# Two MoE routers: each tile of rows gets its own place on the way out, rows are turned first, the modulation's work comes behind, expert slots are shifted by three

## The chip, the cores and the metric

The kernel runs on one core of one Trainium2 chip, in one launch. The metric is device time in microseconds of the whole program. TensorE (PE), VectorE (DVE), ScalarE (ACT), GpSimd (POOL) and SyncE (SP) run programs of their own and meet at semaphores.

## The reference, cut to what matters

Two blocks in sequence. The first has two layers, each a mixer (Fourier and convolution; then attention) and a mixture of experts behind it; the second is one layer with two dense feed-forwards and a mixer between them. The change lies in the mixtures of experts:

```python
def hier_moe(h, grp_w, grp_b, exp_w, exp_b, w_gate, w_up, w_down):
    g_logit = (h @ grp_w) + grp_b                       # 4 groups
    g_idx = argmax(g_logit);  g_prob = softmax(g_logit)[g_idx]
    e_logit = ((h @ exp_w) + exp_b).reshape(n, 4, 8)[g_idx]
    top_v, top_i = lax.top_k(e_logit, 2)
    w = g_prob * softmax(top_v);  e_idx = g_idx * 8 + top_i
    return routed_experts(h, e_idx, w, w_gate, w_up, w_down)

# routed_experts: rows sorted by expert into blocks; per block
#   y = (silu(x @ w_gate[e]) * (x @ w_up[e])) @ w_down[e]
# and out[token] += weight * y
```

There are 768 rows (512 of x, 256 of ctx) in layer 0 and 512 in layer 1, each of 1024 float32; 32 experts, with gate, up and down weights of 1024 x 512 (2 MB each). Layer 1's modulation (scale, shift and gate vectors from `c`, twelve products with units of `mod_w[1]`) is needed only after layer 0, and its units 0 to 3 are computed inside layer 0's router.

## The kernel before, in words

**Layout.** The activations `hT` lie transposed: 8 tiles of 128 features by 768 (or 512) rows. Weights live in `ring`, six slots of 4096 columns (2 MB each); most of the rest is cut from `scr`. There are eight PSUM banks, taken in turn by `ps.take`: an instruction that fills a bank first waits (`ps.ready`) until what its last user left there was taken out.

**The router's job.** After the norm, `pe_router` multiplies `hT` by the router weights and turns the logits, and VectorE (`dve_router`) picks groups and experts, step by step on small tiles. It needs TensorE four more times: counts of rows per expert (`r_n`) and running counts (`r_k`) once the one-hot sum `aa` is there, a broadcast of the experts' places (`r_p`) once `by_expert` is there, and `r_r`, which turns one-hot tiles `oa` and `ob` into the list of rows of each block. From `r_r` VectorE makes `rt`, the row numbers by which POOL gathers.

**Rows on their way out.** Blocks read their rows from HBM, so each tile of 128 rows of `hT` (6 tiles in layer 0, 4 in layer 1) is transposed by TensorE into two banks (`rows(i)`, tag `r_h`), copied by ScalarE into one of two places in `M.hst` and sent by POOL to `hrows` in HBM (`pool_router`, 0.5 MB each). ScalarE copies tile i only when tile i - 2 has landed. When all tiles have landed and `rt` is there, POOL gathers the rows of blocks 0, 1 and 2 (`pool_rows`); TensorE's first transpose of a gathered tile (`x_tr(0)` in `pe_blocks`) begins the expert stage.

**Modulation in layer 0's router.** `mod_load(u)` brings two pieces of 1 MB (half a unit each) into two places of `scr`, each free when TensorE has used what was in it; `pe_mod_pieces` multiplies; ScalarE's `mod_row` copies the result, `pe_mod_turn` turns it in a bank of its own, ScalarE's `mod_columns` copies that. The third x place of the blocks lies over a piece's place, so POOL's gather for block 2 waits until unit 3 is done.

**Orders.** Each engine's program is an order written out by hand. In layer 0 TensorE does: pieces 0, logits, pieces 1, tiles 0 and 1, `r_n` and `r_k`, turn 0, pieces 2, `r_p`, tile 2, turn 1, tile 3, pieces 3, `r_r`, tiles 4 and 5, turns 2 and 3. Layer 1 is the same without the modulation. SP (`sp_moe`, one queue in order) waits for the end of the stage before, then loads router weights and, between the pieces, the fixed weights of expert blocks 0 and 1. Block b's gate, up and down go to slots (3b + kind) mod 6: block 0 has 0, 1, 2, block 1 has 3, 4, 5. From block 2 on POOL fetches weights by an indirect DMA, into slots that TensorE has freed. Ten blocks are wide (128 rows), among them 0, 1 and 3; the other 22 are narrow (64 rows).

**Slots in the stages before.** The Fourier mixer loads raw weights into slots 3, 4 and 5 (its last three jobs into 4, 5 and 3), and 0 to 2 hold tables and split activations to its end. Attention has scratch in slots 0 to 2, output weights in 3 and 4, and the modulation's units 4 to 11 in 5.

**Lines of the profile.** Operations go through small helpers, so the profile's lines are those of helpers: L92 matmul, L95 transpose, L98 and L102 activation and copy on ScalarE, L106 to L120 VectorE's forms, L132 a plain DMA, L135 a gather.

Of the kernel before, what the change touches and what calls it, by code (L numbers as in the profile page):

```python
# [272 lines left out]
def build(nc, I, out, upto=99):  # L273
# [21 lines left out]
    NSLOT, SLOT = 6, 4096  # L295
# [11 lines left out]
    hrows = nc.dram_tensor("hrows", (768, 1024), F32, kind="Internal").ap()  # L307
# [30 lines left out]
    def slot(s, a=0, n=SLOT):  # L338
        return ring[:, s * SLOT + a:s * SLOT + a + n]
# [199 lines left out]
    def pe_mod_turn(e, M, u):  # L539
        l = M.l  # L540
        o = ps.take("mod_t", l, u)
        e.wait_ge(*ps.ready("mod_t", l, u))
        e.wait_ge(*ps.emptied("mod", l, u))
        for j in range(4):
            m = e.matmul(o[:, 2 * j:2 * j + 2], M.row[M.units.index(u) % 2][:, 128 * j:128 * j + 128], group_sum, True, True)
        m.then_inc(*ps.fill("mod_t", l, u))
# [430 lines left out]
    router_in = signal("router_in")  # L977
# [60 lines left out]
                         M.T, None))  # L1038

    def expert_slot(kind, b):  # L1040
        return (3 * b + kind) % NSLOT

    def mod_piece(u, half):
        return lambda kt: moes[0].half[half][:, 512 * (kt % 4):512 * (kt % 4) + 512]

    def sp_moe(e, l):
        M = moes[l]
        e.wait_ge(*act_stage.of(("f", "at")[l]))
        e.wait_ge(*dve_stage.of(("f", "at")[l]))
        e.wait_ge(*ps.filled((st_f, st_at)[l].name, "sum"))  # L1050
        e.dma(M.wr.rearrange("p (k n) -> p k n", k=8), I["router_w"][l]).then_inc(*router_in.up(l, "w", by=16))
        e.dma(M.rb, I["router_b"][l]).then_inc(*router_in.up(l, "b", by=16))

        def fixed(b, *kinds):
            for kind in kinds:
                weights_load(e, expert_slot(kind, b), ("e", l, kind, b),
                             I[f"exp_{('gate', 'up', 'down')[kind]}{l}"].rearrange("(e p) n -> e p n", p=128)[b], 1, 4096)

        def mod_load(u):
            for half in range(2) if l == 0 else ():  # L1060
                wr.take(8 + half, "mod_piece", u, half)
                e.wait_ge(*wr.open("mod_piece", u, half))
                e.dma(M.half[half].rearrange("p (k n) -> p k n", k=4), I["mod_w"][1, u][:, 4 * half:4 * half + 4, :]
                      ).then_inc(*wr.load("mod_piece", u, half))
        mod_load(0)
        fixed(0, 0)
        mod_load(1)
        fixed(0, 1)
        mod_load(2)
        fixed(0, 2)  # L1070
        mod_load(3)
        fixed(1, 0, 1, 2)

        for b in range(FIXED, M.NB):
            for kind in range(3):
                wr.take(expert_slot(kind, b), "e", l, kind, b)
        e.wait_ge(*y_out[0].of(l, 30))
        e.wait_ge(*y_out[1].of(l, 31))
        e.wait_ge(*pool_step.of("further", l))
        for a, n in chunks(M.T):  # L1080
            for i in tiles_of(a, n):
                for q in range(2):
                    r = 768 * q + 128 * i
                    e.dma(moe_y(l, i, q), yrows[r:r + 128, :]).then_inc(*y_in[a].up(l, i, q, by=16))
# [8 lines left out]
    def pe_router(e, l):  # L1093
        M = moes[l]
        NT, T = M.NT, M.T
        if l == 0:
            pe_mod_pieces(e, 0)
        e.wait_ge(*router_in.of(l, "b"))

        for a, n in chunks(T):  # L1100
            o = ps.take("r_l", l, a)
            e.wait_ge(*ps.ready("r_l", l, a))
            for kt in range(8):
                e.wait_ge(*h_ready.of(("hm", l), kt))
                h = 64 * (kt % 2)
                m = e.matmul(o[h:h + 64, 0:n], M.wr[:, 64 * kt:64 * kt + 64], H(kt, a, n), kt < 2, kt >= 6)
            m.then_inc(*ps.fill("r_l", l, a))
        o = ps.take("r_t", l)
        e.wait_ge(*ps.ready("r_t", l))
        e.wait_ge(*dve_step.of("half_sum"))  # L1110
        for a, n in chunks(T):
            e.wait_ge(*ps.emptied("r_l", l, a))
        for i in range(NT):
            m = e.matmul(o[:, 36 * i:36 * i + 36], M.lt[:, 128 * i:128 * i + 128], half_sum, True, True)
        m.then_inc(*ps.fill("r_t", l))

        def rows(i):
            for q in range(2):
                o = ps.take("r_h", l, i, q)
                e.wait_ge(*ps.ready("r_h", l, i, q))  # L1120
                for j in range(4):
                    m = e.transpose(o[:, 128 * j:128 * j + 128], H(4 * q + j, 128 * i, 128), k("id"))
                m.then_inc(*ps.fill("r_h", l, i, q))
        if l == 0:
            pe_mod_pieces(e, 1)
        rows(0)
        rows(1)

        e.wait_ge(*dve_step.of(l, "aa"))
        o = ps.take("r_n", l)  # L1130
        e.wait_ge(*ps.ready("r_n", l))
        e.matmul(o[0:32, 0:32 * NT], k("ones")[:, 0:32], M.AA, True, True).then_inc(*ps.fill("r_n", l))
        o = ps.take("r_k", l)
        e.wait_ge(*ps.ready("r_k", l))
        for s in range(1, NT):
            e.matmul(o[:, 32 * s:32 * NT], k("ones"), M.AA[:, 0:32 * (NT - s)], s == 1, False)
        e.matmul(o[:, 32:32 * NT], k("tri"), M.AA[:, 32:32 * NT], False, True)
        e.matmul(o[:, 0:32], k("tri"), M.AA[:, 0:32], True, True).then_inc(*ps.fill("r_k", l))
        if l == 0:
            pe_mod_turn(e, M.mod, 0)  # L1140
            pe_mod_pieces(e, 2)
        o = ps.take("r_p", l)
        e.wait_ge(*ps.ready("r_p", l))
        e.wait_ge(*dve_step.of(l, "by_expert"))
        e.matmul(o[:, 0:160], k("ones")[0:32, :], M.rows[0:32, :], True, True).then_inc(*ps.fill("r_p", l))
        rows(2)
        if l == 0:
            pe_mod_turn(e, M.mod, 1)
        rows(3)
        if l == 0:  # L1150
            pe_mod_pieces(e, 3)

        o = ps.take("r_r", l)
        e.wait_ge(*ps.ready("r_r", l))
        for q in range(2):
            e.wait_ge(*dve_step.of(l, "oa", q))
            for i in range(NT):
                n = (q * NT + i) * 47
                m = e.matmul(o[:, 0:M.NB], M.oa[q][:, 128 * i:128 * i + 128], M.ob[:, n:n + M.NB], q + i == 0,
                             q == 1 and i == NT - 1)  # L1160
        m.then_inc(*ps.fill("r_r", l))
        for i in range(4, NT):
            rows(i)
        if l == 0:
            pe_mod_turn(e, M.mod, 2)
            pe_mod_turn(e, M.mod, 3)

    def act_router(e, l):
        M = moes[l]
        NT = M.NT  # L1170
        if l == 0:
            mod_row(e, M.mod, 0)
        e.wait_ge(*router_in.of(l, "b"))
        for a, n in chunks(M.T):
            e.wait_ge(*ps.filled("r_l", l, a))
            e.activation(M.lt[:, a:a + n], ps.ap("r_l", l, a)[:, 0:n], ACT.Identity, bias=M.rb).then_inc(
                *ps.empty("r_l", l, a))
        if l == 0:
            mod_row(e, M.mod, 1)

        def rows(i):
            hs = M.hst[:, (i % 2) * 1024:(i % 2) * 1024 + 1024]
            if i >= 2:
                e.wait_ge(*rows_out[i % 2].of(l, i - 2))
            for q in range(2):
                e.wait_ge(*ps.filled("r_h", l, i, q))
                e.copy(hs[:, 512 * q:512 * q + 512], ps.ap("r_h", l, i, q)).then_inc(*ps.empty("r_h", l, i, q))
        rows(0)
        rows(1)
        e.wait_ge(*dve_step.of(l, "w2"))  # L1190
        e.activation(M.gt, M.gt, ACT.Exp)
        e.activation(M.w2, M.w2, ACT.Exp).then_inc(*act_step.up(l, "w2"))
        if l == 0:
            mod_columns(e, M.mod, 0)
            mod_row(e, M.mod, 2)
        rows(2)
        if l == 0:
            mod_columns(e, M.mod, 1)
        rows(3)
        if l == 0:  # L1200
            mod_row(e, M.mod, 3)
        for i in range(4, NT):
            rows(i)
        if l == 0:
            mod_columns(e, M.mod, 2)
            mod_columns(e, M.mod, 3)

    def pool_router(e, l):
        M = moes[l]
        for i in range(M.NT):  # L1210
            e.wait_ge(*ps.emptied("r_h", l, i, 0))
            e.wait_ge(*ps.emptied("r_h", l, i, 1))
            e.dma(hrows[128 * i:128 * i + 128, :], M.hst[:, (i % 2) * 1024:(i % 2) * 1024 + 1024]).then_inc(
                *rows_out[i % 2].up(l, i, by=16))

    def dve_router(e, l):
# [2071 lines left out]
```

## Time and profile before

| | us |
|---|---|
| median of 3 runs | 3353.84 (3346.92 to 3365.6) |
| profiled execution | 3353.96 |
| its span | 3352.2 |
| TensorE busy | 2973.5 (89%) |
| VectorE busy | 1120.3 (33%) |
| ScalarE busy | 740.0 (22%) |
| POOL busy | 460.2 (14%) |

The span is one execution under the profiler. Layer 0's router stands at about 313 to 381 us of it, layer 1's at 1399 to 1443 us; the expert stages follow each. Busy time counts instructions that work, not those that issue DMAs; a matmul's end is modelled. PEclk is the share of TensorE's full clock that was granted. In a timeline row, square brackets hold the idle time before it and what ended it.

### The profile page before, as it was taken

Reading aid. Unit: us, or ns where it says so; the run is one execution under the profiler, and the core shown is the slowest. Engines: PE = TensorE matmul, PEld = TensorE weight load, DVE = VectorE, ACT = ScalarE, POOL = GpSimd, SP = SyncE. Lnnn points to the kernel's source line nnn. Section 1 sums busy time; section 2 is a strip of 40 time slices with the busy share of each in tenths; the row PEclk is TensorE's granted clock in tenths of the full one; section 3 lists DMA queues with packets and bytes.
Section 4 is the critical chain, followed back from the end, with each engine's and each line's share of the span. In section 5 each row is a group of like instructions: output and inputs, shape, how many; then the busy total and the mean of one; then the engine's idle time right before and its main releaser. Section 6 shows DMA issues by size and latency. Waiting matters only on the chain.

```text
span 3352.2 us, 36468 instructions
## 1 busy us (share of the span) xinstructions
PE 2973.5 (89%) x15448; PEld 2039.8 (61%) x15448; DVE 1120.3 (33%) x2211; ACT 740.0 (22%) x1337; POOL 460.2 (14%) x463
## 2 busy tenths in 40 slices
PE   5989798989968899889998968999997678999997
PEld 3777655454457565465454546888646555588876
DVE  3973210000055333310000014323273983432234
ACT  4142110111031143111111113212101333221223
POOL 0000132222210043023323210000000221000000
PEclk8999799999979999889999988999997789999998
DMA  6612799999841231279999961333111002132321
GB/s 241 200 42 115 285 383 399 402 398 396 334 139 52 88 126 51 116 267 401 409 407 403 408 239 51 103 99 101 57 64 73 1 1 101 51 101 91 98 77 56
DMA packets 131881, 622.02 MB, mean 186 GB/s; under 512 B 14063, under 2 KB 85871, under 8 KB 97408
## 3 DMA queue, kind: packets, MB, share of 16 engines
q0 software_dynamic: 40160, 403.75, 29.9%
q1 hardware_dynamic: 90400, 210.87, 18.0%
q10 hardware_dynamic: 1152, 4.98, 0.4%
q8 instruction: 126, 2.06, 0.3%
q14 instruction: 43, 0.35, 0.0%
HBM read 613.25 MB, written 29.36 MB: 192 GB/s over the span
## 4 chain that ended last, share of the span: by engine, by line
PE 60%; DMA 16%; DVE 8%; issue 2%; ACT 1%; POOL 1%; SPq 0%; DVEq 0%; POOLq 0%; ACTq 0%
PE ps L92 58%; DMA ring<-in_exp_up,wix 14%; DVE scr L106 3%; PE ps L95 2%; DVE scr L126 1%; DMA hrows<-scr 1%; DVE scr L120 1%; DVE hT L114 1%; DVE hT_r L106 1%; DVE scr L114 0%; POOL ring L135 0%; DVE hT L129 0%; ACT hT L98 0%; DVE xT L114 0%; DMA scr<-yrows 0%
## 5 line engine op out<-in xcount | busy, mean ns | idle before, releaser
L92 PE MATMUL ps<-ring,scr 128*64 128x512 f32 (+3 forms) x3136 | 734.9, 563 | 67.4 <-DMA ring<-in_exp_up,wix 66.2
L92 PE MATMUL ps<-ring_r 128*128 128x512 f32 (+1 forms) x2544 | 752.7, 377 | 40.2 <-DVE hT_r L106 31.3
L92 PEld LDWEIGHTS ps<-ring_r 128*128 128x128 f32 x2544 | 469.7, 191 | 154.5 <-issue 37.5
L92 PEld LDWEIGHTS ps<-ring,scr 128*64 128x64 f32 (+2 forms) x3136 | 290.1, 154 | 425.5 <-issue 417.9
L92 PE MATMUL ps<-scr,ring 128*128 128x128 f32 (+4 forms) x3744 | 435.5, 306 | 42.1 <-DMA ring<-yrows 20.7
L92 PE MATMUL ps<-hT_r,ring_r 128*128 128x512 f32 (+1 forms) x1224 | 461.0, 377 | 0.0
L92 PEld LDWEIGHTS ps<-scr,ring 128*128 128x128 f32 (+2 forms) x3744 | 396.6, 194 | 83.5 <-issue 71.7
L106 DVE TENSOR_TENSOR scr<-scr,ps 64x512 f32<-64x512 f32 (+1 forms) x72 | 49.7, 690 | 782.5 <-ACT scr L98 439.3
L92 PE MATMUL ps<-scr_r,ring_r 128*128 128x512 f32 x1104 | 259.6, 396 | 0.6 <-DVE scr_r L106 0.6
L92 PEld LDWEIGHTS ps<-hT_r,ring_r 128*128 128x128 f32 x1224 | 234.3, 191 | 40.1 <-issue 2.0
L92 PE MATMUL ps<-ring 128*128 128x512 f32 (+10 forms) x712 | 186.4, 521 | 69.0 <-DVE scr L114 54.7
L92 PEld LDWEIGHTS ps<-scr_r,ring_r 128*128 128x128 f32 x1104 | 207.3, 188 | 51.0 <-issue 1.0
L102 ACT ACTIVATE scr<-ps 128x512 f32<-128x512 f32 (+3 forms) x212 | 111.0, 536 | 540.9 <-PE ps L92 360.7
L106 DVE TENSOR_TENSOR ring_r<-ring,ring_r 128x2048 fp32r<-128x2048 f32 x84 | 189.5, 2287 | 77.1 <-ACT ring_r L102 76.7
L102 ACT ACTIVATE ring_r<-ring 128x2048 fp32r<-128x2048 f32 x88 | 167.0, 1908 | 179.2 <-DMA ring<-in_ffn_w 138.5
L98 ACT ACTIVATE scr<-ps 64x512 f32<-64x512 f32 (+2 forms) x92 | 51.7, 562 | 673.4 <-PE ps L92 673.4
L92 PEld LDWEIGHTS ps<-ring 128*128 128x128 f32 (+3 forms) x712 | 94.6, 191 | 141.1 <-issue 62.0
L103 DVE COPY scr<-ps 128x512 f32<-128x512 f32 (+3 forms) x102 | 54.4, 548 | 282.9 <-PE ps L92 176.8
L95 PEld LDWEIGHTS ps<-KC,scr 64*128 64x128 f32 (+2 forms) x846 | 75.4, 140 | 114.1 <-issue 78.2
L92 PE MATMUL ps<-hT,ring 128*128 128x512 f32 x320 | 142.0, 598 | 0.9 <-DVE hT L114 0.9
L106 DVE TENSOR_TENSOR scr<-hT,ps 128x512 f32<-128x512 f32 x44 | 30.3, 688 | 320.5 <-PE ps L92 320.5
L95 PE MATMUL ps<-KC,scr 64*128 64x64 f32 (+2 forms) x846 | 103.5, 254 | 29.8 <-DMA scr<-hrows,scr 28.2
(140 smaller groups left out, 2466.2 us busy)
## 6 DMA issues: line engine op xcount, KB each, us to landing
ring<-in_ffn_w SPq DMA_DIRECT2D x66, 1024.0 KB, 5.5
ring<-in_mod_w SPq DMA_DIRECT2D x12, 2048.0 KB, 7.9
ring<-in_mod_w SPq DMA_DIRECT2D x16, 1024.0 KB, 5.0
scr<-in_mod_w SPq DMA_DIRECT2D x8, 1024.0 KB, 7.5
ring<-in_exp_gate SPq DMA_DIRECT2D x4, 2048.0 KB, 13.1
ring<-in_exp_up SPq DMA_DIRECT2D x4, 2048.0 KB, 15.7
ring<-in_exp_down SPq DMA_DIRECT2D x4, 2048.0 KB, 20.8
ring<-in_w_in SPq DMA_DIRECT2D x4, 2048.0 KB, 8.1
```

Source lines behind the costliest of these rows:

```text
L92: return self.real.matmul(o, l, r, start=start, stop=stop) if self.real else Quiet()
L95: return self.real.transpose(o, i, identity) if self.real else Quiet()
L98: return self.real.activation(o, i, f, **how) if self.real else Quiet()
L102: return self.real.activation(o, i, ACT.Copy) if self.real else Quiet()
L103: return self.real.tensor_copy(o, i) if self.real else Quiet()
L106: return self.real.tensor_tensor(o, a, b, op) if self.real else Quiet()
L114: return self.real.scalar_tensor_tensor(out=o, in0=a, scalar=s, in1=b, op0=op0, op1=op1) if self.real else Quiet()
L120: return self.real.reciprocal(o, i) if self.real else Quiet()
L126: return self.real.tensor_tensor_scan(o, a, b, first, MUL, ADD) if self.real else Quiet()
```

## The change

Every tile has a place of its own: tiles 0 and 1 in `M.hst` as before, tiles 2 and up in slot 2, which block 1's down weights take after the shift; SP loads those only after the last two tiles have landed. ScalarE's copies wait for no DMA. TensorE turns tiles 0 to 2 before the counts, tile 3 between the counts and `r_p`, the others right behind `r_p`, and behind these turn 0, pieces 2 and turn 1; pieces 3 stand behind `r_r`. ScalarE does all tiles in a row, then the exponentials, then the modulation's copies. Slots are (3b + kind + 3) mod 6: block 0 has 3, 4, 5, block 1 has 0, 1, 2. SP issues two of block 0's weights before it waits for the end of the stage before (up and down in layer 0, down and gate in layer 1).

```diff
     def expert_slot(kind, b):
-        return (3 * b + kind) % NSLOT
+        return (3 * b + kind + 3) % NSLOT
+
+    def row_place(l, i):
+
+        return moes[l].hst[:, 1024 * i:1024 * i + 1024] if i < 2 else slot(expert_slot(2, 1), 1024 * (i - 2), 1024)
...
-        e.wait_ge(*act_stage.of(("f", "at")[l]))
-        e.wait_ge(*dve_stage.of(("f", "at")[l]))
-        e.wait_ge(*ps.filled((st_f, st_at)[l].name, "sum"))
-        e.dma(M.wr.rearrange("p (k n) -> p k n", k=8), I["router_w"][l]).then_inc(*router_in.up(l, "w", by=16))
-        e.dma(M.rb, I["router_b"][l]).then_inc(*router_in.up(l, "b", by=16))
...
+
+        fixed(0, *((1, 2), (2, 0))[l])
+        e.wait_ge(*act_stage.of(("f", "at")[l]))
+        e.wait_ge(*dve_stage.of(("f", "at")[l]))
+        e.wait_ge(*ps.filled((st_f, st_at)[l].name, "sum"))
+        e.dma(M.wr.rearrange("p (k n) -> p k n", k=8), I["router_w"][l]).then_inc(*router_in.up(l, "w", by=16))
+        e.dma(M.rb, I["router_b"][l]).then_inc(*router_in.up(l, "b", by=16))
+
         mod_load(0)
-        fixed(0, 0)
+        fixed(0, (0, 1)[l])
         mod_load(1)
-        fixed(0, 1)
+        fixed(1, 0)
         mod_load(2)
-        fixed(0, 2)
         mod_load(3)
-        fixed(1, 0, 1, 2)
+        fixed(1, 1)
+        for i in (M.NT - 2, M.NT - 1):
+            e.wait_ge(*rows_out[i % 2].of(l, i))
+        fixed(1, 2)
 
...
-        rows(0)
-        rows(1)
+        for i in range(3):
+            rows(i)
...
-        if l == 0:
-            pe_mod_turn(e, M.mod, 0)
-            pe_mod_pieces(e, 2)
+        rows(3)
         o = ps.take("r_p", l)
         e.wait_ge(*ps.ready("r_p", l))
         e.wait_ge(*dve_step.of(l, "by_expert"))
         e.matmul(o[:, 0:160], k("ones")[0:32, :], M.rows[0:32, :], True, True).then_inc(*ps.fill("r_p", l))
-        rows(2)
+        for i in range(4, NT):
+            rows(i)
         if l == 0:
+            pe_mod_turn(e, M.mod, 0)
+            pe_mod_pieces(e, 2)
             pe_mod_turn(e, M.mod, 1)
-        rows(3)
-        if l == 0:
-            pe_mod_pieces(e, 3)
 
...
         m.then_inc(*ps.fill("r_r", l))
-        for i in range(4, NT):
-            rows(i)
         if l == 0:
+            pe_mod_pieces(e, 3)
             pe_mod_turn(e, M.mod, 2)
             pe_mod_turn(e, M.mod, 3)
...
-        def rows(i):
-            hs = M.hst[:, (i % 2) * 1024:(i % 2) * 1024 + 1024]
-            if i >= 2:
-                e.wait_ge(*rows_out[i % 2].of(l, i - 2))
+        for i in range(NT):
             for q in range(2):
                 e.wait_ge(*ps.filled("r_h", l, i, q))
-                e.copy(hs[:, 512 * q:512 * q + 512], ps.ap("r_h", l, i, q)).then_inc(*ps.empty("r_h", l, i, q))
-        rows(0)
-        rows(1)
+                e.copy(row_place(l, i)[:, 512 * q:512 * q + 512], ps.ap("r_h", l, i, q)).then_inc(*ps.empty("r_h", l, i, q))
         e.wait_ge(*dve_step.of(l, "w2"))
         e.activation(M.gt, M.gt, ACT.Exp)
         e.activation(M.w2, M.w2, ACT.Exp).then_inc(*act_step.up(l, "w2"))
         if l == 0:
             mod_columns(e, M.mod, 0)
             mod_row(e, M.mod, 2)
-        rows(2)
-        if l == 0:
             mod_columns(e, M.mod, 1)
-        rows(3)
-        if l == 0:
             mod_row(e, M.mod, 3)
-        for i in range(4, NT):
-            rows(i)
-        if l == 0:
             mod_columns(e, M.mod, 2)
             mod_columns(e, M.mod, 3)
...
-            e.dma(hrows[128 * i:128 * i + 128, :], M.hst[:, (i % 2) * 1024:(i % 2) * 1024 + 1024]).then_inc(
+            e.dma(hrows[128 * i:128 * i + 128, :], row_place(l, i)).then_inc(
                 *rows_out[i % 2].up(l, i, by=16))
```

## Rows read from the trace of the kernel before

**Rows 1.** The page's fourth part: shares of the span in the chain that ended last.

```profile
PE 60%; DMA 16%; DVE 8%; issue 2%; ACT 1%; POOL 1%; SPq 0%; DVEq 0%; POOLq 0%; ACTq 0%
```

**Rows 2.** The chain in order of time, layer 0's router (start, length, what).

```profile
371.99 3.45 issue
376.28 4.34 DMA scr<-hrows,scr
...
380.67 1.98 PE ps L95 x8
```

**Rows 3.** The same chain, layer 1's router.

```profile
1414.71 16.32 DMA hrows<-scr
...
1432.68 5.87 DMA hrows<-scr
...
1439.45 3.48 DMA scr<-hrows,scr
...
1442.97 1.98 PE ps L95 x8
```

**Rows 4.** Timeline of POOL and ScalarE, layer 0 (start, length, operation, idle before).

```profile
352.12 0.54 POOL L132 DMA_DIRECT2D hrows<-scr  x1 [13.63 <-ACT scr L102]
...
362.82 1.09 ACT L102 ACTIVATE scr<-ps 128x512 f32<-128x512 f32 x2 [4.88 <-DMA hrows<-scr]
...
371.46 0.53 POOL L132 DMA_DIRECT2D hrows<-scr  x1 [6.48 <-ACT scr L102]
...
393.03 0.95 POOL L135 DMA_INDIRECT ring<-in_exp_gate,wix  x1 [8.56 <-PE ps L92]
```

**Rows 5.** Timeline of VectorE, where rt is made, layer 0 and layer 1.

```profile
360.82 0.21 DVE L106 TENSOR_TENSOR scr<-scr 128x47 uint32<-128x47 f32 x1
...
1432.67 0.20 DVE L106 TENSOR_TENSOR scr<-scr 128x40 uint32<-128x40 f32 x1
```

**Rows 6.** Timeline of layer 0's router, TensorE and one row of VectorE.

```profile
339.13 3.86 PE L92 MATMUL ps<-scr,KC 128*32 128x192 f32 x16 [2.57 <-DVE scr L106]
...
342.81 1.84 PE L92 MATMUL ps<-AM,scr 128*128 128x2 f32 x8
...
344.58 3.64 PE L92 MATMUL ps<-scr 128*32 128x512 f32 x16
...
348.15 0.90 PE L92 MATMUL ps<-scr,KC 32*128 32x160 f32 x2
...
348.98 1.97 PE L95 MATMUL ps<-KC,hT 128*128 128x128 f32 x8
...
355.14 1.83 DVE L106 TENSOR_TENSOR scr<-KC,scr 128x768 f32<-128x768 f32 x2
...
357.20 2.75 PEld L92 LDWEIGHTS ps<-scr 128*128 128x128 f32 x24 [1.11 <-issue]
```

**Rows 7.** Windows: stretch, its length, busy us (x) per engine, PEclk, DMA share, GB/s.

```profile
290.00:300.00 10.00, 10.00 (x64) 9.04 (x63) 2.98 (x6) 1.68 (x3) 0.00 (x0) 1.00 0.00 0
...
340.00:344.00 4.00, 4.00 (x20) 4.00 (x19) 3.06 (x19) 0.00 (x0) 0.00 (x0) 0.50 1.01 404
...
376.00:380.00 4.00, 0.00 (x0) 0.00 (x0) 0.00 (x0) 0.00 (x0) 3.08 (x3) 0.50 0.24 58
```

**Rows 8.** Landing times from 345 to 380 us: `hrows`, then modulation's pieces.

```profile
DMA to landing us min/median/max: 3.9/10.2/14.4
...
DMA to landing us min/median/max: 6.4/6.8/7.2
```

**Rows 9.** Timeline of TensorE, layer 1: running counts, then `r_p`.

```profile
1417.26 2.22 PE L92 MATMUL ps<-scr,KC 128*32 128x128 f32 x12 [3.89 <-DVE scr L106]
...
1421.48 0.89 PE L92 MATMUL ps<-scr,KC 32*128 32x160 f32 x2 [2.01 <-DVE scr L111]
```

**Rows 10.** Landing times, layer 1: router's two down weights; earlier, attention's modulation units (2 MB).

```profile
DMA to landing us min/median/max: 17.7/26.1/34.5
...
DMA to landing us min/median/max: 7.7/7.8/7.9
```

## The prediction

> **What bounds the kernel now.** I read the page's chain of waits first: the span is TensorE's at 60%, DMA's at 16% [rows 1], the latter nearly all in the expert stages, where narrow blocks wait for streamed weights. The change touches only the two routers, so the next view is the chain around each, in order of time. There the reader is to see that nothing computes: in layer 0 the chain goes from the last tile of rows on its way to `hrows`, through what the page calls issue, to the gather that brings the first expert block's rows back, and only then to TensorE, at 380.67 us [rows 2]; in layer 1 it runs through three row transfers, the longest 16.32 us, and the gather, to 1442.97 us [rows 3].
>
> The timelines say why the rows are late. In layer 0 ScalarE copies tile 4 at 362.82 us, after waiting for the DMA that frees one of the two places, and tile 5 likewise; POOL sends the last at 371.46 [rows 4]. It lands 0.9 us ahead of the gather, the distance that layer 1 shows (1432.68 + 5.87 = 1438.55, gather 1439.45) [rows 3]: 375.4. The other condition for the gather, the list of rows that VectorE makes ("rt"), was there at 361.03 us (360.82 + 0.21) [rows 5]. So in layer 0 the places cost 375.4 - 361.0 = 14.4 us. In layer 1 the last send lands at 1438.55; rt is there at 1432.67 + 0.20 = 1432.87 [rows 3, 5]: 5.7 us. 20.1 us is what the places alone can give back; whatever comes on top must come from an earlier rt.
>
> **Part 1, own places (layer 0).** The copies of tiles 2 to 5 no longer wait for a DMA. What is late next is TensorE, which makes the tiles. From the end of the counting matmuls (339.13 + 3.86, overlapped by the next at 342.81) [rows 6] its new list is: tile 3, the `r_p` matmul, tiles 4 and 5, turn 0, pieces 2, turn 1, `r_r`. Durations are from the same stretch, at the clock that holds there, 0.50 (the 1.2 GHz level) in all four windows from 340 to 356 us, the first of which is shown [rows 7]: a tile 1.97, `r_p` 0.90, a turn 1.84, a pair of pieces 3.64 [rows 6]. So tile 3 ends at 344.8, `r_p` runs to 345.7, tile 5 ends at 349.6. Two copies and 0.5 us to the issue: last send at 350.7 instead of 371.46. Tile 2 goes in front of the counting matmuls, where TensorE was idle 2.57 us [rows 6]; at 1 us (half of a tile's time at the half clock) or even 2 it is hidden. If that cover were gone, 1 us would fall on the chain to rt.
>
> Sends landed in 3.9 to 14.4 us [rows 8]. The long ones ran beside the 6 MB of expert weights that SP issues behind pieces 3. Now SP's queue holds nothing but the two pieces 3 then, so I take 5.5, near the 5.87 of [rows 3]: landed at 356.
>
> **rt.** `r_p` moves from 348.15 to 344.8, which gives 3.3 us to VectorE. But `r_r` needs TensorE too: tiles 4 and 5 and the modulation of piece 2 now stand between. 349.6 + 1.8 (turn 0, whose bank VectorE gives back 3.0 us after `r_p`, in time) + 3.6 + 1.7 = 356.7, against 357.20 before [rows 6]. rt then comes 3.8 us behind, as now (361.03 - 357.20): 360.6, only 0.4 earlier. VectorE's one-hot tiles (before: end 356.97) would come at 353.7 and wait. That is the step which keeps most of `r_p`'s 3.3 us from counting. A waiting turn 0 would hold pieces 2 and `r_r` behind it.
>
> **The gather.** Issue at 360.6 + 0.9 = 361.5 instead of 376.28. Before, it landed in 4.34 us, after SP's queue had run dry: DMA share 0.24 from 376 to 380 [rows 7]. Now it meets traffic. SP issues pieces 3 when pieces 2 have been used (353 and 355), block 1's up weights at 355.5, and its down weights when the last tile has landed, 357: 6.3 MB, at the 404 GB/s of [rows 7] less what POOL's transfers take, busy until about 372. A 0.5 MB transfer of POOL beside SP's traffic took 10.7 us (352.12 to the wait's end at 362.82) and up to 16.32 [rows 3, 4]; alone 4.34 [rows 2]. Ends: 4.3 and 16.3. I take 9, nearest to 10.7 and less because the traffic thins out in its last third: 370.5.
>
> Here a rule can be weighed. The rows show 10.7 us for 0.5 MB beside weights, some 50 GB/s of 404. The Trainium skill ("DMA: Bandwidth & Descriptors", section on queues, rings and completion order) says that each DMA engine alternates between its queues packet by packet, and that a completion increment lands only after earlier writes of that engine, of all its queues. Equal packets would give the gather half of the bandwidth and it would land about 3 us sooner than I take; the rows side with the slower figure. The second half of the rule speaks against moving weights beside the gather.
>
> TensorE's side: pieces 3 land in up to 7.2 us [rows 8], so at 360 and 362.5; two turns at 0.9 (half of 1.84) and ScalarE's copy follow, and TensorE is free at 365. The modulation that now stands behind `r_r` is hidden behind the gather; it would count from a landing later than 368. First transpose in layer 0: 370.5 instead of 380.67, **10.2 us**.
>
> **Part 2, layer 1** (no modulation). Tile 3 stands between counting matmuls (end 1417.26 + 2.22 = 1419.48) and `r_p` at 1421.48 [rows 9]; at half clock it takes 1.97 and fits to within 0.1 us (at most 2 us if its bank were late, none is). rt stays at 1432.9. Sends leave at about 1413.8, 1414.7, 1415.7 and 1422.3. SP issues only three blocks of 2 MB ahead of the row wait; the third landed before at 17.7 us (the shorter of the two of down weights [rows 10]), so near 1419, and the last tile goes alone and lands by 1428. The held down weights follow, 7.8 us when alone [rows 10], gone by 1435.5, when the gather has just begun. It is issued at 1432.9 + 0.9 = 1433.8 and takes 3.5 as now: 1437.3 instead of 1442.97, **5.6 us**. Ends: 3.0, if it meets the last weights and takes 6, and 5.7, the cap.
>
> **Part 3, the early loads and the shift by three.** Two weights of block 0 are issued before the stage's end into slots 4 and 5 (layer 1: 5 and 3), which the stage before has finished with. DMA share is 0.00 from 290 to 300 us [rows 7], and as low in layer 1's stretch, so they land under matmuls that don't touch the queue: 0. Without that cover they would stand ahead of router weights, 5 us each (2 MB at 404 GB/s). Queued behind SP's new waits are only its own later loads; block 1's down weights, the last, are wanted some 30 us after the first transpose. The shift swaps which blocks use which half of the ring; rotation and order stay: 0. What is bound to the first transpose moves with it: the streamed weights of block 2 are released by TensorE (393.03 us, behind block 0's gate) [rows 4], so the whole expert stage starts earlier and is as long as before. ScalarE's exponentials move behind all tiles, to about 352; VectorE wants them after rt: 0.
>
> **Sum.** 10.2 + 5.6 = 15.8 us from the profiled execution's own 3353.96 (span 3352.2 and 1.8 around it): **3338**. That time stands 0.1 us from the median of the three runs, 3353.84.
>
> **Rivals.**
> 1. *The clock doesn't fall.* Granted clock went to 0.50 at about 340 us, after 2.57 us of idle [rows 6, 7]; tile 2 now fills 1 us of it. At full clock (half of each time in [rows 6]) `r_p` runs at 343.5, `r_r` follows VectorE at 352, rt at 355.8, x at 365.7: 15 + 5.6, so 3333. Against: in layer 1 a gap of 3.89 us is cut to 2.9 only.
> 2. *The gather isn't crowded.* It lands in 4.3: 365.8, gain 14.9 + 5.6: 3333. Against: every row beside traffic. (The Trainium skill's alternation between queues, weighed above, would land it between this and the forecast.)
> 3. *The gather is crowded fully.* 16.3: 377.8, gain 2.9; layer 1 at its lower end 3.0: 3348. For: x gets the same queue share as the sends of layer 1; against: traffic ends at 372.
> 4. *Slower.* Pieces 3 hold TensorE ahead of the first transpose. Their load is now issued only after pieces 2 have been used, and TensorE runs in order. Price: 1 us each from a landing past 368 on; slower than before in all past 383 (380.67 + 5.6, less the turns). A transfer at the end of SP's queue took up to 34.5 us [rows 10], from 355 that is 390, 3360. Against: nothing but one half piece is ahead of it; the rows give 7.2.
> 5. *It doesn't do what it says*: rt or TensorE hide as much as the places did. Excluded for layer 0 by the 14.4 us.
>
> **Chances.** Forecast 0.50 (3338 +-4), rival 1 0.15, rival 2 0.15, rival 3 0.14, rivals 4 and 5 0.06. Half a per cent is 16.8 us, about what a measurement tells from no change: faster by more (under 3337.1) holds in most of rivals 1 and 2 and in a third of the forecast, 0.43; within it 0.51; slower 0.06. Range 3325 to 3351: both fast rivals together, at one end, rival 3 at the other, and 3 us for the spread of the runs (3347 to 3366).
>
> **What would show it.** Right: ScalarE's six tiles without a wait for DMA; last send near 351 and 1422; in both layers the gather released by VectorE, not by `hrows`; first transposes near 370 and 1427 (1437 less layer 0's 10). Wrong: gather issued before 358 (the clock), landing under 6 or over 12 us (traffic), the first transpose released by TensorE's own list (pieces 3), or an expert stage longer than before.

## The result, and the profile after

The changed kernel takes 3335.18 us (median of 6 runs, 3329.36 to 3338.44) against 3353.11 for the kernel before on the same chip: ratio 0.9938, 95% interval 0.9922 to 0.9955. A second series gave 3333.88 against 3351.24, ratio 0.9949 (0.9937 to 0.9962). That is 17.4 to 17.9 us less; a time of 3338 us, 15.8 less, had been forecast. The span of the profiled execution is 3327.4 us, 24.8 under the one before.

The chain of waits of the changed kernel around layer 0's first transpose (start, length, what), which answers to [rows 2]:

```profile
354.61 0.22 DVE scr L106
...
355.56 0.20 DVE scr L120
355.78 11.43 DMA scr<-hrows,scr
367.21 0.04 issue
367.26 1.97 PE ps L95 x8
```

The rows' sends are gone from it. VectorE's list now releases the gather; the gather itself has grown from 4.34 to 11.43 us. The DMA view of the same stretch, cut at 360.1 us, says what moved in it. Queue q1 is SP's, q0 is POOL's:

```profile
DMA packets 115, 1.84 MB, mean 439 GB/s; under 512 B 1, under 2 KB 1, under 8 KB 1
q1 hardware_dynamic: 115, 1.84, 102.3%
...
DMA packets 429, 2.46 MB, mean 346 GB/s; under 512 B 213, under 2 KB 213, under 8 KB 301
q1 hardware_dynamic: 156, 2.10, 73.2%
q0 software_dynamic: 273, 0.36, 16.7%
```

From 355.9 to 360.1 us only SP's weights move, nothing of the gather. From 360.1 to 367.2, 88 packets of 4 KB from POOL's queue (301 less 213: rows of this gather and of those behind it) share the engines with SP's 128 of 16 KB (429 less 301).

The chain of waits in layer 1, which answers to [rows 3]:

```profile
1411.15 3.62 PE ps L92 x16
...
1415.49 0.21 DVE scr L106
...
1416.63 3.30 DMA scr<-hrows,scr
1419.97 1.98 PE ps L95 x8
```

POOL's timeline of layer 0 (the last send and the first gather; idle before in brackets) answers to [rows 4]: the last send leaves at 346.76 instead of 371.46.

```profile
346.76 0.53 POOL L132 DMA_DIRECT2D hrows<-ring  x1 [0.45 <-issue]
355.78 1.10 POOL L135 DMA_INDIRECT scr<-hrows,scr  x1 [8.50 <-DVE scr L120]
```

TensorE's timeline of the same stretch answers to [rows 6]. The counts take 2.29 us instead of 3.86, tiles and turns about half of before, and pieces 3, with two waits for their load, stand behind `r_r` (350.73):

```profile
333.99 2.84 PE L95 MATMUL ps<-KC,hT 128*128 128x128 f32 x24
338.53 2.29 PE L92 MATMUL ps<-scr,KC 128*32 128x192 f32 x16 [1.70 <-DVE scr L106]
340.65 1.07 PE L95 MATMUL ps<-KC,hT 128*128 128x128 f32 x8
343.02 0.51 PE L92 MATMUL ps<-scr,KC 32*128 32x160 f32 x2 [1.30 <-DVE scr L111]
...
350.73 3.13 PE L92 MATMUL ps<-scr 128*128 128x47 f32 x24 [1.15 <-DVE scr L106]
354.83 1.94 PE L92 MATMUL ps<-scr 128*32 128x512 f32 x8 [0.97 <-DMA scr<-in_mod_w]
357.32 1.93 PE L92 MATMUL ps<-scr 128*32 128x512 f32 x8 [0.55 <-DMA scr<-in_mod_w]
```

Windows of the changed kernel (columns as in [rows 7], the clock third from the end): it holds through the counts and falls at about 353.

```profile
340.00:344.00 4.00, 2.70 (x23) 2.32 (x22) 2.89 (x16) 1.09 (x2) 0.54 (x1) 1.00 0.98 397
344.00:348.00 4.00, 3.74 (x37) 2.57 (x35) 3.58 (x12) 3.73 (x8) 1.06 (x2) 1.00 0.88 356
...
356.00:360.00 4.00, 3.45 (x16) 1.02 (x13) 2.30 (x8) 0.60 (x1) 1.91 (x2) 0.50 1.02 438
```

Cut at the issue of the router's weights, the first transpose and the first load of results (the stages' borders), the 24.8 us between the two profiles are: layer 0's router 13.4 (68.1 to 54.7), first expert stage 6.0 (549.0 to 542.9), layer 1's router 5.6 (43.8 to 38.2), second expert stage 1.9, attention -2.0, the rest 0. The 6.0 are not shown to be the change's: another profile of the kernel before has 542.8 there.

### The profile page after: what moved, and what is told of

Same layout as the page of the kernel before. It is cut to its first block, busy times and chain, and to the rows that moved or that the text cites. A ratio compares the mean times of both kernels' runs of the same rounds, so it can differ in the third digit from the quotient of the medians.

```text
span 3327.4 us, 36466 instructions
## 1 busy us (share of the span) xinstructions
PE 2977.4 (89%) x15448; PEld 2045.4 (61%) x15448; DVE 1121.0 (34%) x2211; ACT 739.6 (22%) x1337; POOL 460.1 (14%) x463
## 3 DMA queue, kind: packets, MB, share of 16 engines
q0 software_dynamic: 40160, 403.75, 30.0%
## 4 chain that ended last, share of the span: by engine, by line
PE 69%; DMA 14%; DVE 12%; issue 2%; ACT 1%; POOL 1%; SPq 0%; DVEq 0%; POOLq 0%; ACTq 0%
PE ps L92 67%; DMA ring<-in_exp_up,wix 12%; DVE scr L106 4%; DVE scr L114 2%; PE ps L95 2%; DVE scr L126 1%; DVE hT L114 1%; DVE scr L120 1%; DVE hT_r L106 1%; ACT scr L98 0%; DMA scr<-hrows,scr 0%; DVE scr L117 0%; POOL ring L135 0%; DVE ring_r L106 0%; DMA KC<-in_kon 0%
## 5 line engine op out<-in xcount | busy, mean ns | idle before, releaser
L102 ACT ACTIVATE scr<-ps 128x512 f32<-128x512 f32 (+3 forms) x200 | 104.1, 531 | 519.7 <-PE ps L92 352.9
L106 DVE TENSOR_TENSOR scr<-scr 128x512 f32<-128x512 f32 (+9 forms) x328 | 122.6, 395 | 18.7 <-ACT scr L98 12.6
```

The lines of the kernel that those rows point to most:

```text
L102: return self.real.activation(o, i, ACT.Copy) if self.real else Quiet()
L106: return self.real.tensor_tensor(o, a, b, op) if self.real else Quiet()
```

## Experiments

All are read in the same way: "router" is the time from the issue of the router's weights to the first transpose of gathered rows, from one profile each; times are medians with the ratio to the kernel before on the same chip. The table stands ahead, the reasons below.

| kernel | rt | last send | gather issued | landed in | router, layer 0 | router, layer 1 | us | ratio (95%) |
|---|---|---|---|---|---|---|---|---|
| before | 48.4 | 58.9 | 63.7 | 4.4 | 68.1 | 43.8 | 3353.11 | |
| before, again | 53.5 | 57.4 | 65.0 | 4.3 | 69.3 | 43.9 | 3355.99 | 1.0008 (0.9998 to 1.0019) |
| changed | 42.3 | 34.2 | 43.2 | 11.5 | 54.7 | 38.2 | 3335.18 | 0.9938 (0.9922 to 0.9955) |
| changed, again | 42.7 | 34.5 | 43.7 | 11.2 | 54.9 | 38.5 | 3333.88 | 0.9949 (0.9937 to 0.9962) |
| places alone | 52.0 | 55.7 | 60.1 | 8.8 | 68.9 | 43.8 | 3353.79 | 0.9991 (0.9979 to 1.0004) |
| early loads alone | 50.2 | 56.3 | 60.2 | 4.3 | 64.4 | 38.2 | 3348.83 | 0.9992 (0.9975 to 1.0009) |
| all but own places | 45.9 | 40.6 | 50.4 | 11.1 | 61.5 | 38.7 | 3341.63 | 0.9978 (0.9966 to 0.9989) |
| all but early loads | 43.3 | 37.0 | 50.4 | 10.9 | 61.3 | 44.2 | 3350.44 | 0.9995 (0.9977 to 1.0013) |
| all but modulation behind | 48.3 | 42.3 | 51.8 | 8.7 | 60.5 | 38.6 | 3339.20 | 0.9955 (0.9939 to 0.9972) |
| all but tile 2 first | 44.3 | 37.9 | 46.3 | 12.2 | 58.4 | 38.8 | 3335.97 | 0.9964 (0.9950 to 0.9978) |
| changed, gather alone | 42.4 | 34.2 | 43.3 | 4.4 | 49.5 | 38.5 | 3330.57 | 0.9941 (0.9928 to 0.9954) |
| the same, turns later | 43.4 | 34.9 | 44.4 | 4.6 | 49.0 | 38.1 | 3328.47 | 0.9937 (0.9923 to 0.9951) |

(Columns 2 to 4 are layer 0's, in us behind the issue of the router's weights; the fifth is the time from the gather's issue to the first transpose. For "gather alone" it is to SP's release, since TensorE came later. The ratios are to the kernel before on the same chip at the same time: 3350.97 us for early loads alone and for all but own places, early loads and tile 2 first; 3351.24 for both repeats, the gather alone and turns later; 3353.85 for places alone and all but modulation behind.)

**All but own places.**

```diff
+            if i >= 2:
+                e.wait_ge(*rows_out[i % 2].of(l, i - 2))
             for q in range(2):
                 e.wait_ge(*ps.filled("r_h", l, i, q))
```

> The changed kernel with the old waits back: ScalarE copies tile i only when tile i-2 has landed, as with two places; all else stays. Measured by the length of each router, from the issue of the router's weights to the first transpose of gathered rows: before 68.1 us (layer 0) and 43.8 (layer 1), changed kernel 54.7 and 38.2. Theory A (the places gave the time): layer 0's last two tiles are copied 6 us or more later than at 346, the last send lands after rt, and the router takes 59 to 62 us; layer 1 stays within 0.5 us of 38.2, since its sends land long before rt either way; total +5 to +7 us on the changed kernel. Theory B (SP's new order and the early loads gave it, by making landings short): both routers stay within 1 us of 54.7 and 38.2 and the total doesn't move.

Theory A holds in layer 0: 61.5 against 54.7. ScalarE's timeline of this run shows the waits; each also holds the copies that TensorE needs next (TensorE idles 1.81 us for one of them, last row), so rt moves too, by 3.6 us:

```profile
350.64 2.31 ACT L102 ACTIVATE ring<-ps 128x512 f32<-128x512 f32 x4 [8.51 <-DMA hrows<-scr]
355.20 1.09 ACT L102 ACTIVATE ring<-ps 128x512 f32<-128x512 f32 x2 [2.25 <-DMA hrows<-ring]
356.65 1.09 ACT L102 ACTIVATE ring<-ps 128x512 f32<-128x512 f32 x2 [0.36 <-DMA hrows<-ring]
...
351.29 2.37 PE L95 MATMUL ps<-KC,hT 128*128 128x128 f32 x12 [1.81 <-ACT ring L102]
```

In layer 1 the places are worth 0.5 us at most. The median is 6 to 8 us over the changed kernel's, as theory A said.

**Early loads alone**, in the kernel before:

```diff
-        return (3 * b + kind) % NSLOT
+        return (3 * b + kind + 3) % NSLOT
...
+        fixed(0, *((1, 2), (2, 0))[l])          # ahead of the stage's waits
...
-        fixed(0, 0)
+        fixed(0, (0, 1)[l])
         mod_load(1)
-        fixed(0, 1)
+        fixed(1, 0)
         mod_load(2)
-        fixed(0, 2)
         mod_load(3)
-        fixed(1, 0, 1, 2)
+        fixed(1, 1, 2)
```

> The kernel before with SP's part alone: two of block 0's weights issued before the stage's end, slots shifted by three, router order on the other engines and the two places as before, block 1's up and down issued without a hold. Theory A (places): layer 0's router 65 to 68 us, layer 1's 43, total within 3 us of before. Theory B (SP's order): layer 1's router falls to 38 to 39, as its queue holds 8 MB and not 12 when the sends go out and the last send lands ahead of rt; layer 0's to 62 or less; total -8 us or more. A mixture is likely by the queue's arithmetic: layer 0 near 65, layer 1 near 38.5, total -8.

Layer 1 has its whole gain, 38.2, with two places and the old orders; layer 0 has 3.6 to 4.9 of 13 to 15. So the mixture holds for the routers. The total moved less than expected: 9 to 10 us in the routers, 2.1 in the median, with an interval that reaches from -8 to +3 us.

**All but early loads.**

```diff
-        fixed(0, *((1, 2), (2, 0))[l])
...
-        fixed(0, (0, 1)[l])
+        fixed(0, 0)
         mod_load(1)
-        fixed(1, 0)
+        fixed(0, 1)
         mod_load(2)
+        fixed(0, 2)
         mod_load(3)
-        fixed(1, 1)
+        fixed(1, 0, 1)
```

> The changed kernel without the early loads: SP issues all of block 0's weights behind the router's weights in the old order, block 1's gate and up next, down behind the landing of the last tiles. Theory A (own places make the landing time of a send unimportant): layer 0's router 54.7 to 58 us, the gather landing in 12 to 15 us instead of 11.4, layer 1's 38 to 40. Theory B (early loads): layer 1's router goes back to 42 us or more, layer 0's to 60 or more; total +9 us on the changed kernel.

Theory B holds: layer 1 is back at 44.2, layer 0 at 61.3. The total rose by more than the 9 us expected: 16.6 over the changed kernel on the same chip, with runs from 3336 to 3356 us. The chain in layer 0 shows what the early loads did there. The last send takes 12.51 us to land and releases the gather 7 us behind rt; in the changed kernel SP, which waits for that landing, went on 4.3 us behind the last send's issue (346.76 to 351.04).

```profile
353.11 12.51 DMA hrows<-ring
...
366.54 10.84 DMA scr<-hrows,scr
```

The chain in layer 1: rt is as early as ever, and the gather, alone in 3.3 to 3.6 us, lands beside the held weights:

```profile
1427.53 0.21 DVE scr L106
...
1429.69 8.05 DMA scr<-hrows,scr
1437.79 1.98 PE ps L95 x8
```

**Places alone**, in the kernel before:

```diff
-            hs = M.hst[:, (i % 2) * 1024:(i % 2) * 1024 + 1024]
-            if i >= 2:
-                e.wait_ge(*rows_out[i % 2].of(l, i - 2))
+            hs = row_place(l, i)
...
-        fixed(1, 0, 1, 2)
+        fixed(1, 0, 1)
+        for i in (M.NT - 2, M.NT - 1):
+            e.wait_ge(*rows_out[i % 2].of(l, i))
+        fixed(1, 2)
```

> The kernel before with own places alone (slot 5 for tiles 2 and up, block 1's down weights held until the last tiles have landed), TensorE's and ScalarE's order, slots and SP's other loads as before. Theory A (places are worth 14.4 and 5.7 us): layer 0's router 54 to 56 us, layer 1's 38 to 39, total -18 us. Theory G (the orders are needed too): tiles 4 and 5 still stand behind r_r on TensorE, so their sends leave at 49 us or later and land beside traffic at 55 to 60, layer 0's router 60 to 66 us (6 us of gain or less); layer 1, whose sends leave at 25 us, lands at 33 and gains 4 to 6 us; total -6 to -12 us.

Neither theory: nothing is gained in either layer (68.9, 43.8), nor in the median (3353.79 against 3353.85). TensorE's timeline of layer 0 shows one half, pieces 3 with waits for their load, then `r_r` (inside the second row), and tiles 4 and 5 last:

```profile
356.42 1.93 PE L92 MATMUL ps<-scr 128*32 128x512 f32 x8 [1.27 <-DMA scr<-in_mod_w]
359.73 7.22 PE L92 MATMUL ps<-scr 128*32 128x512 f32 x32 [1.38 <-DMA scr<-in_mod_w]
366.74 3.65 PE L95 MATMUL ps<-KC,hT 128*128 128x128 f32 x16
```

The chain of the same run shows the other half, in layer 0 and in layer 1: the gather, released 4 to 5 us sooner, pays them back beside the weights that the landing has released. The places come with this hold, since they lie in the slot of block 1's down weights; this run tests the two together.

```profile
375.93 8.77 DMA scr<-hrows,scr
...
1439.10 8.15 DMA scr<-hrows,scr
1447.26 0.04 issue
1447.30 1.98 PE ps L95 x8
```

**All but modulation behind.**

```diff
+        if l == 0:
+            pe_mod_turn(e, M.mod, 0)
+            pe_mod_pieces(e, 2)
         rows(3)
...
         if l == 0:
-            pe_mod_turn(e, M.mod, 0)
-            pe_mod_pieces(e, 2)
             pe_mod_turn(e, M.mod, 1)
+            pe_mod_pieces(e, 3)
```

with ScalarE's order to match. (TensorE's order is shown.)

> The changed kernel (own places, early loads, hold) with the modulation back ahead of what VectorE waits for: turn 0 and pieces 2 before tile 3 and r_p, pieces 3 before r_r. Theory G (the modulation's place on TensorE is worth what rt gains: pieces 3 make r_r wait for a DMA): rt 47 to 52 us behind the router's weights instead of 42.3, with r_r behind a wait for the mod_w load; the sends still leave by 42, and the gather is released by rt; layer 0's router 57 to 62 us, total +3 to +6 us on the changed kernel. Theory A alone (only the places count): rt hidden or unmoved, router within 1 us of 54.8. Layer 1's router 38.2 in both.

Theory G's times hold: rt 48.3, router 60.5, median 3 to 4 us over the changed kernel's. Its reason holds in part. Pieces 2, not pieces 3, wait for their load, ahead of `r_p` (TensorE's timeline), and behind that wait the clock was 0.50, where it had been 1.00:

```profile
346.12 1.32 PE L92 MATMUL ps<-scr 128*32 128x512 f32 x8 [2.32 <-DMA scr<-in_mod_w]
```

**All but tile 2 first.**

```diff
-        for i in range(3):
-            rows(i)
+        rows(0)
+        rows(1)
...
-        rows(3)
+        rows(2)
...
-        for i in range(4, NT):
+        for i in range(3, NT):
```

> The changed kernel with tile 2 turned behind the counts and tile 3 behind r_p, so that TensorE idles 2.6 us instead of 1.7 before the counts, as it did before. Theory C (1 us of transposes in that gap keeps the clock): granted clock falls to 0.50 near 340 us, rt comes 4 to 6 us later than at 354.8 and layer 0's router takes 59 to 61 us; total +4 to +6. Theory D (the clock stays up for another reason or is chance): clock 1.00 through 350, rt within 1 us of 354.8, router within 1.5 us of 54.7. Layer 1 unchanged within 1 us in both.

In between the two theories: the clock fell 25 us behind the router's weights and was back at 35, rt came 2.1 us later, the router took 58.4. Over all twelve profiles, the counts ran at full clock (2.29 us) in six of seven with tile 2 in the gap (2.54 without early loads) and in one of five without it (2.29 in places alone; else 2.63 to 4.19). So full clock was more frequent with a tile in the gap, and not certain; with one profile for most kernels more is not shown. The time of this run is not to be told from the changed kernel's (intervals overlap).

**Both kernels again.**

> The kernel before, once more, for its profile: how much its stages move from run to run. If the first expert stage (first transpose to the first load of results) is again near 549 us, the 543 of the changed kernel's profile is an effect of the change; if it lies between 543 and 549, it is the spread of runs. The clock before the counts should fall again (26 to 28 us behind the router's weights).

> The changed kernel once more. Theory C (the transposes of tile 2 keep the clock): granted clock 1.00 until 38 us behind the router's weights, layer 0's router 54 to 56 us. Theory D (chance): the clock falls at 28 us or so, as in the variant without early loads, whose TensorE order is the same; rt then comes 1 to 4 us later and the router takes 56 to 59 us. Layer 1's router 38.2 in both. Time about 5 to 6 tenths of a per cent under before.

The first expert stage took 542.8 and 544.9 us: the 6.0 lie within the spread. The changed kernel kept its clock until 40 us behind the router's weights, as theory C said, with a router of 54.9; but the run without early loads, with the same order on TensorE, had lost it at 29. In the repeat of the kernel before, the clock fell at 29 us and TensorE waited 5.2 us for pieces 3 ahead of `r_r`. In the profile on which I predicted only a weight load waited, 1.15 us (the last row here; the others are from the repeat):

```profile
356.72 1.31 PE L92 MATMUL ps<-scr 128*32 128x512 f32 x8 [3.27 <-DMA scr<-in_mod_w]
360.00 7.22 PE L92 MATMUL ps<-scr 128*32 128x512 f32 x32 [1.96 <-DMA scr<-in_mod_w]
...
355.54 0.15 PEld L92 LDWEIGHTS ps<-scr 128*32 128x32 f32 x4 [1.15 <-DMA scr<-in_mod_w]
```

**The gather alone, and the turns later.**

```diff
-        fixed(1, 1)
         for i in (M.NT - 2, M.NT - 1):
             e.wait_ge(*rows_out[i % 2].of(l, i))
-        fixed(1, 2)
+        e.wait_ge(*xg_in[0].of(l, 0))
+        fixed(1, 1, 2)
```

> The changed kernel, but SP holds block 1's up and down weights until the first gather has landed. Theory E (the gather's 11.4 us in layer 0, against 3.3 to 4.3 without traffic, are the weights beside it): it lands in 4 to 7 us, the first transpose is then bound by TensorE's pieces 3 and turns (50 us behind the router's weights), layer 0's router takes 50 to 52 us instead of 54.7, layer 1's 38.2 as now, total -3 to -5 us on the changed kernel. Theory F (the traffic doesn't matter, the first gather is slow by itself): landing stays at 11 us. If block 1's weights come too late, TensorE waits ahead of block 1, 17 us behind the first transpose.

Theory E. The router took 49.5, a little under the 50 to 52 expected. The gather issued at 355.89 had landed when SP went on at 360.29, and the first transpose followed TensorE's turns (timelines of SP and TensorE):

```profile
358.60 3.58 PE L92 MATMUL ps<-AM,scr 128*128 128x2 f32 x16
...
360.29 0.33 SPq L132 DMA_DIRECT2D ring<-in_exp_up  x1
...
362.04 1.95 PE L95 MATMUL ps<-KC,scr 128*128 128x128 f32 x8
```

For the second kernel, `pe_mod_turn` 2 and 3 and their copies go behind block 0's gate and up.

> The kernel with the gather alone and, on top, the modulation's turns 2 and 3 and their copies behind expert block 0's gate and up. If TensorE's turns (3.6 us at the half clock) bound the first transpose once the gather is fast, the router takes 1 to 3 us less than with the gather alone: 48 to 50 us, total -5 to -7 us on the changed kernel, and two turns of 0.5 to 0.9 us each are paid inside block 0's stretch. If the gather binds, no difference.

The router took 49.0, only 0.5 less: pieces 3 end at 361.7 there and the gather 1.1 us later, so the gather binds again. On one chip the medians are 3333.88 (changed), 3330.57 and 3328.47. The last is the fastest kernel tried, 5.4 us under the change; of the two, neither is shown faster than the other.

## Why the prediction was right, and where it wasn't

**The numbers.** 15.8 us were forecast; 17.4 to 17.9 were measured, in the range. Layer 1's 5.6 is 5.6 (43.83 - 38.24). Layer 0's 10.2 is 13.4, of two errors with opposite signs: rt came 5.7 us earlier than forecast, the gather took 2.4 longer. That the total still lay near the forecast is in part luck.

**rt** was mis-sized: 48.0 us behind the router's weights forecast (360.6 - 312.6), 42.3 measured. I had carried the half clock of one profile through TensorE's whole list. Rival 1, full clock, was right on it (355.8 - 312.6 = 43.2), and my own sign for it came: the gather was issued before 358, at 355.78. The forecast put the clock at 4.8 us of rt (360.6 against rival 1's 355.8). Where it did fall with the same order, in the run without early loads, it was back after some 7 us and rt came at 43.3, so there it cost about 1 us. The other part is what I wrote off at "only 0.4 earlier": with the modulation ahead of what VectorE waits for, rt comes 5.6 to 6 us later in its own experiment.

**The gather** was under-sized: 9 us taken, 11.4 measured. That the traffic of block 1's weights does it is shown by holding them: 4.4. The figure of [rows 4], 10.7, would have been nearer than my allowance for thinning traffic. Equal shares, 6 us, don't fit the 11.4, for two reasons that the packets in the traces show. The gather's first row starts 4.4 us behind its issue (1.8 when SP's loads are held), and then POOL's packets are of 4 KB and SP's of 16: 88 against 128 in number, but 0.36 MB against 2.10. The Trainium skill's alternation of queues by packets ("DMA: Bandwidth & Descriptors", section on queues, rings and completion order) fits these rows in kind; my step from there to half of the bandwidth took the packets as equal in size, and they aren't. Nor is this gather the 0.5 MB that I compared with a send. It asks for 128 rows and skips those that the block doesn't have: in all twelve profiles POOL's queue moved 403.75 MB, which is, to 0.05 MB, its 180 weight loads, ten sends, and 2560 rows gathered and 2560 scattered (1280 rows, two experts each), with nothing for the places of a block that stay empty. In the run without early loads POOL's queue had begun 59 packets of 4 KB (202 less 143) between the first gather's issue and its landing, so that gather moves at most 0.24 MB:

```profile
DMA packets 467, 4.58 MB, mean 423 GB/s; under 512 B 143, under 2 KB 143, under 8 KB 202
q0 software_dynamic: 170, 0.24, 6.0%
```

**"20.1 us is what the places alone can give back"** was wrong as a statement on cause. It is the gap between two releases in the trace of before, and taking one away made the next thing late at once: alone the places gave nothing. In layer 0 three parts are each worth about 6 to 7 us of the router when the others are there (places 6.8, early loads 6.6, modulation behind 5.8), and they sum to more than the whole 13 to 15 because each removes what would hide another. In layer 1 I booked the gain to the places and the early loads at 0; it is the reverse. With 4 MB less in SP's queue two places suffice (38.7 and 38.2), and without the early loads own places don't help (44.2, 43.8). "Land under matmuls: 0" priced the loads where they went. The shorter queue that they left stood in the working ("only three blocks of 2 MB ahead of the row wait"), but its gain was credited to the places.

**Rivals.** 2 (gather not crowded) and 3 (fully crowded) are out. 4: pieces 3 end at 359.3 and the turns at 362.8, 4.5 us ahead of the transpose; they bind once the gather is quick. 5 is out for the whole change, but the reason I gave against it, the 14.4 us between two releases, was none: with the places alone, rt and the gather hid all that they gave. The missing waits and VectorE as the gather's releaser came as written. The last send left as forecast in layer 1 (23.3 us behind the router's weights) and 4 us sooner than forecast in layer 0 (346.76, not 350.7). That forecast too stood on the half clock; where the clock did fall with the same order, without early loads, the send left 2.8 us later than in the changed kernel (37.0 against 34.2).

**Open.** Early loads alone and the change without them moved the routers by 10 and 7 us and the median by 2.1 and 0.5; a profile is one execution, its first expert stage spreads over 8 us in the twelve (540.6 to 549.0) and its start over 5. Whether something after the routers takes the rest back is not settled. Nor is what keeps the clock in the gap. Attention took 470.9 to 473.0 us in the eight profiles with the changed orders and 469.0 to 470.5 in the four with the old ones, up to some 3 us that go against the gain. In windows of 20 us from 60 to 120 us behind its start the clock was 1.00 in both profiles of the kernel before and 0.80 to 0.91 in at least two of the three in all ten others, early loads alone and places alone among them; the cause is not known.

## What to carry to other kernels

The gap between the last and the last-but-one release bounds what removing that one wait can bring; it doesn't say that it will, and with the places alone nothing came. Undo each part before crediting it. When a latency-bound read stands behind a stage's end, count what is queued beside it: 4 MB of weights, first used 21 us behind the first transpose, cost a gather of at most 0.24 MB 7 us, and moving 4 MB ahead of the stage gave layer 1's router its whole gain. On an in-order engine, work that can wait for a load goes behind the instructions others wait for.

## What the runs showed of the hardware

The first gather of a stage (at most 59 rows of 4 KB in layer 0, 36 in layer 1) landed in 3.3 to 4.6 us alone and in 8.1 to 12.2 beside SP's weight loads, in twelve profiles. Its first row started 1.8 us behind the issue alone and 4.2 to 5.0 beside them. From then on, in the changed kernel, POOL's queue moved 0.36 MB in packets of 4 KB while SP's moved 2.10 MB in packets of 16 KB. TensorE's clock fell to its 1.2 GHz level before or in the counts behind 2.5 us of idle in four profiles of five, behind 1.7 us in one of seven; where it came back, that took 7 to 17 us (17 in the one profile on which I predicted), and in places alone, where it fell later, it was still at 0.50 after 28.
